# All modulation dot products moved beside tokens and filter spectra, and each slot of the joined stage reordered: evictions and weights first, norm steps behind

## The chip, the cores and the metric

One core of a Trainium2 chip. The metric is the time of one launch in device microseconds (us), median of several executions. The kernel is one program of ten stages with a barrier of all engines between two stages; instructions of one engine run in the order written, and semaphores order the engines against each other.

## What is computed

Two transformer-like blocks on 1024 tokens of width 1024, in float32: a first block (16 meta tokens, a sparse attention, a gated recurrence, an output product, a layer norm), then a block with latent attention over the tokens and 256 context rows, then one with long convolutions whose filters are made on the fly and transformed to spectra. What matters here:

```
a  = silu(gate_proj(h)) * features            # per unit "G"
x  = layer_norm(alpha*h + a @ w_out)          # units "OUT", chain norm1
shift, scale, gate = silu(c) @ ada_w[i] + ada_b[i]     # i = 0, 1: 48 columns of 128
a2 = rmsnorm(x)*g*(1+scale) + shift           # chain norm2, needs the modulation
ac = the same for the context rows with silu(c_ctx)    # i = 0 only
cq, ckv, k_rope, gate = split(a2 @ mla_w_in)  # then rmsnorm of cq and ckv, q, k, v
spec = rfft(filters * decay)                  # independent of everything above
```

The modulation is 48 dot products per partition: `ada_w[:, m, :]` is a 128 x 1024 tile (512 KB), and tile m against the condition row gives column m of `K.ada`. The first 16 columns are needed for the context rows too, which makes 64 products.

## The kernel before

**Stage one, `stage_spectra_tokens` (line 449).** TensorE multiplies the tokens with two small weights, tile by tile (9 tiles, `token_products`, lines 711 and 713), then makes the filters (`hidden_out`, line 736) and transforms them (line 766). The loop over `it` from 0 to 3 takes one order and one half of the channels; `it` is order-major (`o, h = it // 2, it % 2`). VectorE multiplies the filters with `decay` out of PSUM (line 632), forms radix sums (`radix`, lines 422 to 433), and takes the latents of each token tile (`take_latent`, 577 to 580, then `norm_latents`, 584 to 592). ScalarE makes `decay`, 8 tiles of 128 x 1024 (line 665), empties the value banks (672) and the spectrum banks (688) into a ring of four tiles `kst`. The sync queue (SP) stores values (537), spectra (550), and in `it == 3` reloads the block's input, one of 8 pieces beside each of the first 8 spectrum stores (555). TensorE runs three steps ahead of the emptied banks; the transposes of the latents (723) wait for `normed`.

**The joined stage, `stage_gates_to_keys` (line 1727).** 141 units in one list `UNITS`, each one PSUM bank of products: units 0 to 7 `G` (gates of half 0), 8 to 15 `OUT`, 16 to 23 and 24 to 31 the same for half 1, 32 to 34 the context rows, 35 to 49 and 50 to 64 the input projections of both halves, from 65 (`QN`) on queries, keys and values. A unit of 8 k-tiles is 24 matmuls, three per k-tile (`split_product`, lines 313 to 315: float32 as two parts). Four banks turn over. Each unit has a weight tile of its own (`WeightStream`, line 1565): SP loads 512 KB into one of two raw slots, ScalarE rounds it (1592) once the unit two back is done, GpSimd subtracts to get the rest (1598), and TensorE waits for that. So per unit there is a fixed chain: products of unit u, then rounding and rest of tile u+2, and that has until the end of unit u+1.

The order of each engine's work is written out by hand: for every unit u ScalarE does first the norm steps listed for u, then empties unit u's bank, then rounds tile u+2; VectorE does the modulation work and norm steps of u, then its part of unit u; GpSimd does its adds for u, then the rest of tile u+2. Norm steps stand in `CHAIN` (norm1 and norm2 for each half, `HalfNorm`, line 1609: ScalarE squares, GpSimd adds, TensorE sums over partitions in `total`, line 1647, VectorE and ScalarE make the root): `center` 18 and 34, `sums1` 20 and 36, `sums2` 25 and 40, `apply` 27 to 31 and 41 to 45. TensorE comes to `total` right behind unit `sums1` or `sums2` and waits there for all seven adds.

The modulation (`AdaSums`, line 1676) stands in this stage: `A1` takes columns 0 to 15, in pairs (1 MB loads), with both conditions (lines 1717 and 1720) beside units 0 to 11, `A2` columns 16 to 47 beside units 49 to 64. SP's loads of the pairs stand between its loads of the weight tiles, and each waits for the pair two back.

Of the kernel before, what the change touches and what calls it, by code (L numbers as in the profile page):

```python
# [18 lines left out]
F32 = mybir.dt.float32  # L19
# [6 lines left out]
P = 128  # L26
# [421 lines left out]

def stage_spectra_tokens(K):

    nc, dram = K.nc, K.dram
    decay = K.view(1024, 8192).rearrange("p (t c) -> p t c", t=8)
# [5 lines left out]
    delta = K.view(23744, 1024)  # L458
# [25 lines left out]
    latents_out = K.sem("latents_stored")  # L484

# [25 lines left out]
    with nc.Block() as block:  # L511

        @block.sync
        def _(sp):
# [11 lines left out]
            for dst, src in [(w_fb[0:64, :, :, :], dram["filt_w_out"]),  # L526
                             (delta, bass.AP(dram["delta"].tensor, 0, [[0, P], [1, D]])), (K.ident, dram["ident"]),
                             (K.kvg_row, bass.AP(dram["kv_g_row"].tensor, 0, [[0, P], [1, P]]))]:
                sp.dma_start(dst, src).then_inc(loads, 16)
            sp.dma_start(mats[:, 0:NSPEC0 * P], dram["dft_spec"][:, 0:NSPEC0 * P]).then_inc(mats_loaded, 16)  # L530
# [16 lines left out]
            for n, (it, s, p, row, _) in enumerate(spec_order):  # L547

                sp.wait_ge(sp_ev, n + 1)
                sp.dma_start(dram["spec"][it, row, :, :], kst[:, n % 4, :]).then_inc(stored[n % 4], 16)  # L550
                if it == 3 and s == 0 and n % 17 < 8:

                    sp.wait_ge(hd_ev, 64)
                    k = n % 17
                    sp.dma_start(K.view(1024, 8 * E).rearrange("p (k n) -> p k n", k=8)[:, k, :],
                                 dram["hT"][:, k, :]).then_inc(h_loaded, 16)
# [5 lines left out]
        def _(dve):  # L562
# [5 lines left out]
            def make_weights():  # L568
                dve.wait_ge(loads, 16 * 4)
# [45 lines left out]
            for it in range(4):  # L615
                o, h = it // 2, it % 2
                for s in range(2):
                    if it == 0 and s == 1:

                        radix(K, dve, link, lambda t2: ed[:, 0, 2 * t2:2 * t2 + 2, :], Y[0], tmp, y_ready[0])  # L620
                        for t in range(1, 9):
                            take_latent(t)
                        norm_latents()
# [4 lines left out]
                    for t in range(TT):  # L628
                        dve.wait_ge(hd_mm, n + 1)
                        if n == 0:  # L630
                            dve.wait_ge(decay_ready, 1)
                        ins = v.tensor_tensor(ed[:, s, t, :], K.bank(n % 4),
                                              decay[:, t, h * HALF:(h + 1) * HALF], ALU.mult)
# [9 lines left out]
                for s in range(2):  # L643
# [5 lines left out]
                    radix(K, dve, link, lambda t2: ed[:, s, 2 * t2:2 * t2 + 2, :], Y[s], tmp, y_ready[s])  # L649

        @block.scalar
        def _(act):
# [9 lines left out]
            act.wait_ge(loads, 16 * 4)  # L662
# [3 lines left out]
            ins.then_inc(decay_ready, 1)  # L666
            for t in range(9):
# [9 lines left out]
            for n in range(len(spec_order)):  # L677
                if n == 3:
# [4 lines left out]
                    nc.scalar.activation(cT[:, L:E], K.bank(2, META), ACT.Copy).then_inc(t_ev, 1)  # L683
                act.wait_ge(sp_mm, n + 1)
# [6 lines left out]
        def _(pe):  # L691
# [34 lines left out]
            def hidden_out(it, parts=(0, 1)):  # L726
                o, h = it // 2, it % 2
# [881 lines left out]
class HalfNorm:  # L1609
# [3 lines left out]
    def __init__(self, K, tag, x, kt, dim, banks, sq, rstd, acc, widths=(HALF, HALF)):  # L1613
# [3 lines left out]
        self.sums = [K.bank(b, n) for b, n in zip(banks, widths)]  # L1617
# [27 lines left out]
    def total(self, pe, j):  # L1645
        pe.wait_ge(self.added, (self.kt - 1) * (j + 1))
        self.K.nc.tensor.matmul(self.sums[j], self.K.ones, self.acc[:, 0:self.widths[j]], start=True, stop=True)\  # L1647
# [26 lines left out]


class AdaSums:


    def __init__(self, K, tag, first, pairs, with_ctx, w_at, cond_at, sums_at, spare=None):
        self.spare = spare  # L1680
        self.K, self.first, self.pairs, self.with_ctx = K, first, pairs, with_ctx
        self.w = [K.view(w_at + 2048 * s, 2048).rearrange("p (t k) -> p t k", t=2) for s in range(2)]
        self.cond = [K.view(cond_at + D * n, D) for n in range(2)]
        self.both = K.view(cond_at, 2 * D)
        self.sums = [K.view(sums_at + 4 * s, 4).rearrange("p (t v) -> p t v", v=2) for s in range(2)]
        self.rows_in, self.rows_ready = K.sem(f"{tag}_conditions_loaded"), K.sem(f"{tag}_conditions_ready")
        self.loaded = [K.sem(f"{tag}_ada_loaded{s}") for s in range(2)]
        self.used, self.ctx_used, self.copied = (K.sem(f"{tag}_ada_{n}") for n in ("used", "ctx_used", "copied"))

    def load_rows(self, sp):  # L1690
        sp.dma_start(self.both, bass.AP(self.K.dram["cond"].tensor, 0, [[0, P], [1, 2 * D]])).then_inc(self.rows_in, 16)

    def silu(self, act):
        act.wait_ge(self.rows_in, 16)
        self.K.nc.scalar.activation(self.both, self.both, ACT.Silu).then_inc(self.rows_ready, 1)

    def load(self, sp, g):
        if g < self.pairs:
            if g >= 2:
                sp.wait_ge(self.used, 2 * (g - 1))  # L1700
            at = self.first + 2 * g
            sp.dma_start(self.w[g % 2], self.K.dram["ada_w"][:, at:at + 2, :]).then_inc(self.loaded[g % 2], 16)

    def work(self, dve, g):
        v = self.K.nc.vector
        at, sums = self.first + 2 * g, self.sums[g % 2]
# [1608 lines left out]
```

## Time and profile before

| | us |
|---|---|
| median of 3 runs | 3032.46 (3028.85 to 3034.70) |
| profiled execution, its time | 3030.52 |
| its span, first to last instruction | 3028.7 |
| PE busy in it | 2740.2 (90%) |
| DVE busy in it | 1878.6 (62%) |
| mean granted TensorE clock | 0.953 |

Times below count from the start of the span. Stage one runs from 0 to 376, the joined stage from 1081. In the views PE is TensorE, DVE VectorE, ACT ScalarE, POOL GpSimd, SP the sync queue. A row of the order of time has the start, the duration, engine, line, operation, names, and in brackets how long the engine was idle before it and what ended that. The profile names PEclk the granted clock, in shares of 2.4 GHz.

### The profile page before, as it was taken

What the parts mean: (1) busy time and instruction counts of PE and PEld (TensorE: products, weight loads), DVE (VectorE), ACT (ScalarE), POOL (GpSimd) and SP (SyncE); (2) the same over time, 40 slices, a digit from 0 to 9 for tenths busy, and PEclk for the clock granted to TensorE, in tenths of its full rate; (3) what the DMA queues carried; (4) which work ended last, traced back from release to release, by engine and by line L of the source; (5) the groups of instructions that cost most, each with busy time, mean ns of one, the idle gap of its engine ahead of it and who ended that gap; (6) DMA issues with size and microseconds to landing.
All of it is one profiled execution on the core that took longest, in us unless ns stands there. A gap on an engine that the chain in (4) does not pass through costs nothing. (4 is left out here: it accounts for less than half of the span.)

```text
span 3028.7 us, 30579 instructions
## 1 busy us (share of the span) xinstructions
PE 2740.2 (90%) x11377; PEld 1868.9 (62%) x11377; DVE 1878.6 (62%) x2979; ACT 894.8 (30%) x1519; POOL 810.6 (27%) x486
## 2 busy tenths in 40 slices
PE   7999989978689978788999999996999998999967
PEld 3544434547456556566778899995778885444456
DVE  6256239999576668755851555554785533888564
ACT  2111121100344332435434565552332211111122
POOL 0000000004021135565432233324542220343234
PEclk9999999989889989899999999997999999999979
DMA  4211411110100034143856323214421123111043
GB/s 151 81 70 63 142 62 42 35 43 1 56 1 1 1 146 160 63 142 127 280 188 206 93 57 91 68 38 134 144 84 49 42 70 149 59 59 59 28 167 111
DMA packets 109560, 269.78 MB, mean 89 GB/s; under 512 B 18464, under 2 KB 34664, under 8 KB 105001
## 3 DMA queue, kind: packets, MB, share of 16 engines
q1 hardware_dynamic: 109418, 267.90, 26.5%
q8 instruction: 88, 1.44, 0.2%
q14 instruction: 54, 0.44, 0.0%
HBM read 206.87 MB, written 60.99 MB: 88 GB/s over the span
## 5 line engine op out<-in xcount | busy, mean ns | idle before, releaser
L313 PE MATMUL psum<-part,part 128*128 128x512 f32 (+1 forms) x1984 | 766.9, 387 | 94.4 <-POOL part L1598 49.2
L314 PE MATMUL psum<-part,part 128*128 128x512 f32 (+1 forms) x1984 | 744.4, 375 | 0.0
L315 PE MATMUL psum<-part,part 128*128 128x512 f32 (+1 forms) x1984 | 742.9, 374 | 0.0
L1598 POOL TENSOR_TENSOR part<-arena,part 128x1024 fp32r<-128x1024 f32 (+1 forms) x149 | 370.8, 2489 | 712.3 <-ACT part L1592 712.3
L313 PEld LDWEIGHTS psum<-part,part 128*128 128x128 f32 x1984 | 379.8, 191 | 183.4 <-POOL part L1598 95.5
L314 PEld LDWEIGHTS psum<-part,part 128*128 128x128 f32 x1984 | 380.4, 192 | 71.3 <-issue 3.2
L315 PEld LDWEIGHTS psum<-part,part 128*128 128x128 f32 x1984 | 379.2, 191 | 71.6
L221 PE MATMUL psum<-arena 128*128 128x512 f32 (+1 forms) x672 | 232.4, 505 | 17.3 <-DMA arena<-in_w_f 10.0
L1592 ACT ACTIVATE part<-arena 128x1024 fp32r<-128x1024 f32 (+1 forms) x149 | 155.4, 1043 | 262.9 <-PE psum L315 183.0
L1135 POOL TENSOR_TENSOR arena<-arena 128x256 f32<-128x256 f32 x56 | 38.2, 682 | 705.2 <-PE psum L1148 705.2
L2413 DVE TENSOR_REDUCE arena<-psum 128x1 f32<-128x1280 f32 x64 | 95.5, 1492 | 175.9 <-PE psum L2365 175.9
L766 PE MATMUL psum<-arena 128*128 128x512 f32 x464 | 200.6, 593 | 0.7 <-issue 0.7
L221 PEld LDWEIGHTS psum<-arena 128*128 128x128 f32 x672 | 114.3, 193 | 136.0 <-issue 127.9
L2887 PE MATMUL psum<-arena 128*128 128x512 f32 x448 | 192.9, 592 | 0.0
L920 DVE TENSOR_SCALAR_CACHE_REDUCE arena<-arena 128x384 bf16<-128x384 f32 (+2 forms) x198 | 173.9, 940 | 1.9 <-PEq L100 0.8
L766 PEld LDWEIGHTS psum<-arena 128*128 128x128 f32 x464 | 87.7, 190 | 112.7 <-issue 112.7
L2887 PEld LDWEIGHTS psum<-arena 128*128 128x128 f32 x448 | 85.1, 190 | 107.1 <-issue 107.1
L2873 PE MATMUL psum<-arena 128*128 128x512 f32 x256 | 118.5, 623 | 27.4 <-DVE arena L2974 14.2
L2454 ACT ACTIVATE part<-psum 128x512 fp32r<-128x512 f32 (+1 forms) x192 | 93.6, 522 | 134.5 <-PE psum L2374 134.4
L2426 DVE TENSOR_TENSOR part<-psum,part 128x512 fp32r<-128x512 f32 (+1 forms) x192 | 109.1, 595 | 37.3 <-ACT part L2454 37.3
L2902 ACT ACTIVATE arena<-psum 128x512 f32<-128x512 f32 x64 | 36.1, 599 | 301.7 <-POOL arena L2996 174.0
L2873 PEld LDWEIGHTS psum<-arena 128*128 128x128 f32 x256 | 50.7, 200 | 94.4 <-issue 80.8
(311 smaller groups left out, 4074.4 us busy)
## 6 DMA issues: line engine op xcount, KB each, us to landing
arena<-in_ada_w SPq DMA_DIRECT2D x24, 1024.0 KB, 5.3
arena<-in_w_hy SPq DMA_DIRECT2D x40, 512.0 KB, 3.2
scratch_spec<-arena SPq DMA_DIRECT2D x68, 256.0 KB, 2.0
arena<-scratch_spec SPq DMA_DIRECT2D x12, 1024.0 KB, 5.3
arena<-in_w_gate SPq DMA_DIRECT2D x16, 512.0 KB, 4.1
arena<-in_w_out SPq DMA_DIRECT2D x16, 512.0 KB, 4.0
arena<-in_w_mgate SPq DMA_DIRECT2D x16, 512.0 KB, 4.1
arena<-in_w_mout SPq DMA_DIRECT2D x16, 512.0 KB, 3.5
```

Source lines behind the costliest of these rows:

```text
L221: last = nc.tensor.matmul(acc, slot_w[s][:, c], rhs(k, n0, n), start=(k == 0), stop=(k == kt - 1))
L313: nc.tensor.matmul(acc, a_hi, b_hi, start=start, stop=False)
L314: nc.tensor.matmul(acc, a_hi, b_lo, start=False, stop=False)
L315: return nc.tensor.matmul(acc, a_lo, b_hi, start=False, stop=stop)
L766: last = nc.tensor.matmul(K.bank(4 + n % 4), mats[:, m * P:(m + 1) * P], Y[s][:, y, :], start=(q == 0), stop=(q == len(blocks) - 1))
L920: last = v.tensor_scalar(junk[:, (block_at(n + 2) - block_at(2)):(block_at(n + 3) - block_at(2))], s, against if isinstance(against, float ...
L1592: self.K.nc.scalar.activation(self.hi[i % 2][:, 0:n], self.raw[i % 2][:, 0:n], ACT.Copy)\
L1598: self.K.nc.gpsimd.tensor_tensor(self.lo[s][:, 0:n], self.raw[s][:, 0:n], self.hi[s][:, 0:n].bitcast(F32), ALU.subtract).then_inc(self.spl ...
L2413: v.reduce_max(top[:, i % 2:i % 2 + 1], K.psum[:, at:at + LC], AX_X).then_inc(topped, 1)
L2426: v.tensor_tensor(pT_lo[g % 2][:, k0:k0 + cnt, cols], chunk_bank(n, cnt).rearrange("p (k n) -> p k n", n=P), pT_hi[g % 2][:, k0:k0 + cnt, ...
L2873: last = nc.tensor.matmul(K.bank(4 * (g % 2) + b), fwd[:, m * P:(m + 1) * P], tile(it, PAIRS[n], part), start=(part == 0), stop=(part == 1))
L2887: last = nc.tensor.matmul(K.bank(n), inv[:, m * P:(m + 1) * P], tile(it, r, part), start=(q == 0), stop=(q == len(blocks) - 1))
```

## The change

Three parts.

**Modulation into stage one.** `AdaSums` is rewritten: one class, single columns (512 KB loads, two slots at 7168 and 8192), sums written straight into `K.ada`. Columns 0 to 23 (0 to 15 with both conditions) are worked on VectorE beside token tiles 1 to 8, three per tile behind that tile's `take_latent`: five products of 128 x 1024. `norm_latents` stays behind them. Columns 24 to 47 are worked behind the radix sums of `it` = 1, 2 and 3 (7, 7 and 10 of them). SP issues each load behind a value store or a spectrum store, and waits first for the column two back. The condition rows (1 MB) and two columns are loaded before the first DFT matrices. The bias and the three `modA` vectors are made at the end of the stage. To make room, `decay` is 8 tiles of 128 x 512 and made twice: for channels of half 0 at the start, for half 1 at spectrum n = 18 (16 activations of 256 columns), and the loop over `it` is half-major. In `it == 3` input pieces 0 to 2 are loaded beside the first three stores, pieces 3 to 7 beside the last five (n % 17 from 12 on), behind the last column.

**Modulation out of the joined stage.** A1, A2, their loads, the condition rows and `modulated` go. `NC` (the context norm) is scaled at units 12 and 13 and rounded at 29 and 30 instead of 13 and 16.

**The slots of the joined stage.** For every u each engine now empties unit u (or does its part of it) and rounds or subtracts tile u+2 first, and does the norm steps of u behind that. The numbers in `CHAIN` go down: by one for `center`, `stats1`, `scale`, and the centring is split over two units; by two for `sums2` of half 0, `stats2` and `apply` of half 0. `total` of norm1 comes behind unit 19 and 35 instead of 20 and 36, of norm2 behind 23 and 39 instead of 25 and 40.

```
 def stage_spectra_tokens(K):
-    decay = K.view(1024, 8192).rearrange("p (t c) -> p t c", t=8)
+    decay = K.view(1024, 4096).rearrange("p (t c) -> p t c", t=8)
+    A = AdaSums(K, [m for t in range(8) for m in (2 * t, 2 * t + 1, 16 + t)] + list(range(24, 48)), 16, (7168, 8192),
+                5120, K.view(45568, D))
+    ADA_LATE = {1: range(24, 31), 2: range(31, 38), 3: range(38, 48)}
...                                   # SP
+            A.load_rows(sp)
+            A.load(sp, 0)
+            A.load(sp, 1)
             sp.dma_start(mats[:, 0:NSPEC0 * P], dram["dft_spec"][:, 0:NSPEC0 * P]).then_inc(mats_loaded, 16)
...
                 sp.dma_start(dram["vN"][0:n, t, :], vN_slot[t % 3][0:n, :]).then_inc(v_out[t % 3], 16)
+                if t:
+                    for i in range(3 * t - 3, 3 * t):
+                        A.load(sp, i + 2)
...
+                late = ADA_LATE.get(it, [])
+                if 2 <= n % 17 < 2 + len(late):
+                    A.load(sp, late[n % 17 - 2] + 2)
+                if it == 3:
+                    ks = [n % 17] if n % 17 < 3 else [n % 17 - 9] if 12 <= n % 17 < 17 else []
+                    for k in ks:
+                        sp.wait_ge(hd_ev, 64)
+                        if k >= 3:
+                            sp.wait_ge(A.used, 48)
...                                   # VectorE
                         for t in range(1, 9):
                             take_latent(t)
+                            for i in range(3 * t - 3, 3 * t):
+                                A.work(dve, i)
                         norm_latents()
...
                     radix(K, dve, link, lambda t2: ed[:, s, 2 * t2:2 * t2 + 2, :], Y[s], tmp, y_ready[s])
+                for i in ADA_LATE.get(it, []):
+                    A.work(dve, i)
 def stage_gates_to_keys(K):
-    CHAIN = {0: dict(center=18, sums1=20, stats1=21, scale={21: [0, 1], 22: [2, 3, 4], 23: [5, 6, 7]}, sums2=25, stats2=26,
-                     apply={27: [0], 28: [1, 2], 29: [3, 4], 30: [5, 6], 31: [7]},
-                     add1={18: [1, 2, 3], 19: [4, 5, 6, 7]}, add2={22: [1], 23: [2, 3, 4], 24: [5, 6, 7]}),
+    CHAIN = {0: dict(mean=17, center={17: [0, 1, 2, 3], 18: [4, 5, 6, 7]}, sums1=19, stats1=20,
+                     scale={20: [0, 1], 21: [2, 3, 4], 22: [5, 6, 7]}, sums2=23, stats2=24,
+                     apply={24: [0], 25: [1, 2], 26: [3, 4], 27: [5, 6], 28: [7]},
+                     add1={17: [1, 2, 3], 18: [4, 5, 6, 7]}, add2={20: [1], 21: [2, 3, 4], 22: [5, 6, 7]}),
...
```

## Rows read from the trace of the kernel before

**Rows 1.** Busy time of each engine in three stretches of the joined stage.

```profile
core 0: us, PE busy (x) PEld busy (x) DVE busy (x) ACT busy (x) POOL busy (x), PEclk, DMA share, GB/s
1090.00:1218.00 128.00, 110.42 (x434) 86.66 (x435) 116.69 (x143) 42.90 (x63) 67.33 (x32) 0.91 0.45 163
1218.00:1328.70 110.70, 89.67 (x343) 69.20 (x342) 80.72 (x65) 44.52 (x58) 63.25 (x33) 0.89 0.26 81
...
1391.00:1545.00 154.00, 144.32 (x589) 112.30 (x589) 129.41 (x126) 69.93 (x91) 70.49 (x31) 0.97 0.67 230
```

**Rows 2.** Waits of PE, joined stage: us in total, times, longest.

```profile
PE psum L313 <- POOL part L1598: 45.3, 20, 6.1
PE psum L313 <- DVE part L2109: 11.7, 2, 9.6
```

**Rows 3.** PE in order of time: two rows of steady work, 42 matmuls apart.

```profile
1107.44 0.40 PE L313 MATMUL psum<-part,part 128*128 128x512 f32 x1
...
1117.20 0.39 PE L313 MATMUL psum<-part,part 128*128 128x512 f32 x1
```

**Rows 4.** PE in order of time: units 14, 20, 23 and 36 start after a wait.

```profile
1193.60 0.79 PE L313 MATMUL psum<-part,part 128*128 128x512 f32 x1 [5.75 <-POOL part L1598]
...
1236.28 0.80 PE L313 MATMUL psum<-part,part 128*128 128x512 f32 x1 [6.09 <-POOL part L1598]
...
1262.48 0.79 PE L313 MATMUL psum<-part,part 128*128 128x512 f32 x1 [5.98 <-POOL part L1598]
...
1353.19 0.79 PE L313 MATMUL psum<-part,part 128*128 128x512 f32 x1 [5.66 <-POOL part L1598]
```

**Rows 5.** Dot products, and rests of weights: duration min/median/max in ns.

```profile
L1720 DVE CUSTOM_DVE_ANT_0 arena<-arena x48: 1212/1226/3469, 1103.3 to 1548.5; 128x1024 f32<-128x1024 f32 x48
...
L1598 POOL TENSOR_TENSOR part<-arena,part x149: 1851/2409/3385, 1086.9 to 3000.9; 128x1024 fp32r<-128x1024 f32 x141, 128x768 fp32r<-128x768 f32 x8
```

**Rows 6.** In order of time, half 0's norm1: unit 17 emptied, squares, adds, sum.

```profile
1218.26 0.60 ACT L2072 ACTIVATE arena<-psum 128x512 f32<-128x512 f32 x1 [3.95 <-PE psum L315]
...
1224.23 2.44 ACT L1627 ACTIVATE arena<-arena 128x512 f32<-128x512 f32 x4 [4.42 <-DVE arena L2153]
...
1236.19 6.55 POOL L1643 TENSOR_TENSOR arena<-arena 128x512 f32<-128x512 f32 x4
...
1243.24 1.02 PE L1647 MATMUL psum<-arena 128*128 128x512 f32 x2
```

**Rows 7.** Stage one in order of time, decay to the first transforms; then `it` = 2.

```profile
34.33 8.42 ACT L665 ACTIVATE arena<-arena 128x1024 f32<-128x1024 f32 x8
...
42.88 3.08 DVE L632 TENSOR_TENSOR arena<-psum,arena 128x512 f32<-128x512 f32 x5 [5.54 <-ACT arena L665]
...
62.41 1.22 DVE L433 SCALAR_TENSOR_TENSOR arena<-arena 128x1024 f32<-128x1024 f32 x1
...
121.14 0.16 DVE L577 TENSOR_SCALAR arena<-psum 128x4 f32<-128x4 f32 x1 [7.97 <-PE psum L711]
...
124.43 2.44 DVE L592 SCALAR_TENSOR_TENSOR arena<-arena 16x128 f32<-16x128 f32 x9
...
222.06 0.69 DVE L632 TENSOR_TENSOR arena<-psum,arena 128x512 f32<-128x512 f32 x1 [14.64 <-PE psum L736]
...
49.92 0.81 PE L711 MATMUL psum<-arena 128*128 128x132 f32 x2
...
122.62 5.39 PE L766 MATMUL psum<-arena 128*128 128x512 f32 x12 [0.73 <-issue]
...
129.03 7.03 PE L766 MATMUL psum<-arena 128*128 128x512 f32 x16
```

**Rows 8.** Loads of stage one: count, KB each, median us from issue to landing.

```profile
arena<-in_hT SPq DMA_DIRECT2D x15, 520.0 KB, 4.0
...
arena<-in_w_idx SPq DMA_DIRECT2D x2, 512.0 KB, 3.4
```

**Rows 9.** The end of stage one: SP's last spectrum stores, PE's next product.

```profile
363.18 10.62 SPq L550 DMA_DIRECT2D scratch_spec<-arena  x4
...
380.13 4.63 PE L221 MATMUL psum<-arena 128*128 128x512 f32 x5 [7.31 <-DMA arena<-in_w_idx]
```

More of the change, by code:

```diff
@@ L446, in chain, with __init__, load_rows, silu @@
     return link
+class AdaSums:
+    def __init__(self, K, order, with_ctx, w_at, cond_at, spare):
+        self.K, self.order, self.with_ctx, self.spare = K, order, with_ctx, spare
+        self.w = [K.view(at, D) for at in w_at]
+        self.cond = [K.view(cond_at + D * n, D) for n in range(2)]
+        self.both = K.view(cond_at, 2 * D)
+        self.rows_in, self.rows_ready = K.sem("ada_conditions_loaded"), K.sem("ada_conditions_ready")
+        self.loaded = [K.sem(f"ada_loaded{s}") for s in range(2)]
+        self.used, self.ctx_used = K.sem("ada_used"), K.sem("ada_ctx_used")
+    def load_rows(self, sp):
+        sp.dma_start(self.both, bass.AP(self.K.dram["cond"].tensor, 0, [[0, P], [1, 2 * D]])).then_inc(self.rows_in, 16)
+    def silu(self, act):
+        act.wait_ge(self.rows_in, 16)
+        self.K.nc.scalar.activation(self.both, self.both, ACT.Silu).then_inc(self.rows_ready, 1)
+    def load(self, sp, i):
+        if i < len(self.order):
+            if i >= 2:
+                sp.wait_ge(self.used, i - 1)
+            sp.dma_start(self.w[i % 2], self.K.dram["ada_w"][:, self.order[i], :]).then_inc(self.loaded[i % 2], 16)
+    def work(self, dve, i):
+        product = self.K.nc.vector.tensor_tensor_reduce
+        m, w = self.order[i], self.w[i % 2]
+        if i == 0:
+            dve.wait_ge(self.rows_ready, 1)
+        dve.wait_ge(self.loaded[i % 2], 16 * (i // 2 + 1))
+        if m < self.with_ctx:
+            n = sum(t < self.with_ctx for t in self.order[:i])
+            if n:
+                dve.wait_ge(self.ctx_used, n)
+            product(self.spare, w, self.cond[1], 1.0, 0.0, ALU.mult, ALU.add, self.K.ada[:, m, 1:2])\
+                .then_inc(self.ctx_used, 1)
+            dve.wait_ge(self.ctx_used, n + 1)
+        product(w, w, self.cond[0], 1.0, 0.0, ALU.mult, ALU.add, self.K.ada[:, m, 0:1]).then_inc(self.used, 1)
 def stage_spectra_tokens(K):
     nc, dram = K.nc, K.dram
-    decay = K.view(1024, 8192).rearrange("p (t c) -> p t c", t=8)
+    decay = K.view(1024, 4096).rearrange("p (t c) -> p t c", t=8)
     ed = K.view(9216, 8192).rearrange("p (s t c) -> p s t c", s=2, t=8)
@@ L683, in _ @@
                     nc.scalar.activation(cT[:, L:E], K.bank(2, META), ACT.Copy).then_inc(t_ev, 1)
+                if n == 18:
+                    act.wait_ge(hd_ev, 32)
+                    for t in range(TT):
+                        for q in range(2):
+                            ins = nc.scalar.activation(decay[:, t, 256 * q:256 * q + 256], delta_late[q], ACT.Exp,
+                                                       scale=K.col("neg_t", t))
+                    ins.then_inc(decay_ready, 1)
                 act.wait_ge(sp_mm, n + 1)
@@ L1616, in __init__ @@
         self.acc = K.view(acc, max(widths))
-        self.sums = [K.bank(b, n) for b, n in zip(banks, widths)]
+        self.banks, self.sums = banks, [K.bank(b, n) for b, n in zip(banks, widths)]
         self.rstd = [K.view(at, n) for at, n in zip(rstd, widths)]
@@ L1673, in __getitem__ @@
         return self.tiles[k][:, columns]
[L1676 to L1706, printed above, removed]
-        if g == 0:
-            dve.wait_ge(self.rows_ready, 1)
-        dve.wait_ge(self.loaded[g % 2], 16 * (g // 2 + 1))
-        if g >= 2:
-            dve.wait_ge(self.copied, g - 1)
-        for t in range(2):
-            w = self.w[g % 2][:, t, :]
-            if self.with_ctx:
-                if 2 * g + t:
-                    dve.wait_ge(self.ctx_used, 2 * g + t)
-                v.tensor_tensor_reduce(self.spare(g), w, self.cond[1], 1.0, 0.0, ALU.mult, ALU.add,
-                                       sums[:, t, 1:2]).then_inc(self.ctx_used, 1)
-                dve.wait_ge(self.ctx_used, 2 * g + t + 1)
-            v.tensor_tensor_reduce(w, w, self.cond[0], 1.0, 0.0, ALU.mult, ALU.add, sums[:, t, 0:1])\
-                .then_inc(self.used, 1)
-        dve.wait_ge(self.used, 2 * g + 2)
-        n = 2 if self.with_ctx else 1
-        v.tensor_copy(self.K.ada[:, at:at + 2, 0:n], sums[:, :, 0:n]).then_inc(self.copied, 1)
```

298 lines of the change are left out of this document (133 added, 165 removed).

## The prediction, made before the changed kernel ran

> **What bounds the kernel now.** I read first the busy time by stretches, and there the joined stage alone, since every edit but those in stage one lies in it. TensorE does a third of its work of the stage while units 0 to 17 run, and over 128.0 us it is busy 110.4; over units 18 to 31 it is busy 89.7 of 110.7, and from unit 41 to the queries 144.3 of 154.0, with granted clocks of 0.91, 0.89 and 0.97 [rows 1]. The steady pitch of a matmul is (1117.20 - 1107.44) / 42 = 0.2324 us [rows 3], so a unit of 24 is 5.58, units 0 to 17 are 100.4 and cost 128.0. The stage is bound by TensorE where it runs, but 27.6 us are lost in that stretch: 17.6 idle, 10.0 at the low clock. The waits say on whom: 45.3 us in 20 waits on GpSimd's rest of a weight tile [rows 2]. The order of time shows the second half of the price: behind a wait of 5 to 6 us the first matmul lasts 0.79 instead of 0.40 [rows 3, 4], the 1.2 GHz level. With some four such starts in 0 to 17 (start of the stage included) 10.0 us are 2.5 each.
>
> Why is the rest late? Not GpSimd: it is busy 67 of 128 us, VectorE 117 of 128 [rows 1]. A dot product takes 1.23 us, and 3.4 when it meets a rest of weights; a rest 2.4, up to 3.4 [rows 5]. SP waits for the dot products (two pairs back) before it issues the next weight load, so a late VectorE makes late weights.
>
> **Removing A1.** Nothing but gates and products is left beside units 0 to 15. A rest of tile u+2 ends about 0.6 + 1.0 + 2.4 = 4.0 us behind unit u by its chain, and TensorE wants it at 5.58: 1.6 to spare, 0.6 with a slow rest. I take all waits away but the first (weights and h must land). The wait of 11.7 - 9.6 = 2.1 at the second matmul group [rows 2] goes too: that weight tile stood behind 1 MB of condition rows. One cold start of 2.5 stays. Units 0 to 17 and two small sums: 100.4 + 2.5 + 1.0 = 103.9 against 128.0 + 0.7 for the sum that now comes one unit earlier: **-25**.
>
> **The slots.** I wrote both orders out as one list per engine. Before: norm steps of u, empty u, round u+2. After: empty u, round u+2, norm steps of u, and the numbers one lower. The lists come out the same. What really moves is what went down by more than one, or stayed behind: the centring is in two parts, so unit 18 is emptied between them, the context rounding leaves unit 16, `apply` comes sooner, and above all TensorE's `total` stands one unit sooner (norm1) or two and one (norm2). TensorE waits there for seven GpSimd adds.
>
> Half 0, norm1, from the end of unit 17 (unit 17 is emptied at 1218.3): squares begin 6 us later; the last four adds took 6.55 and ended at 1242.7, 24.5 later; the sum ran at 1243.24, right behind unit 20 [rows 6], so before it cost no wait. After: four squares are done at +8.7, unit 18 is emptied and tile 20 rounded at once, so GpSimd has no hole before rest 20; VectorE's second four centrings come behind unit 18's three operations, and the adds end between +20 (adds at 1.3, about half of a rest's 2.4 for half its columns [rows 5]) and +23 (at 1.64 as in the row). Unit 19 ends at +11.2. TensorE waits 9 to 12 us, starts cold, and ends unit 20 at 0.7 + 5.6 + 2.5 behind the sum, +29 to +32, where before unit 20 and its sum ended at +26 (1244.3). Tile 23 comes 19 us behind the end of unit 20 in both lists (1262.48 less 1243.2 [rows 4, 6]); `total` of norm2 waits some 9 us more at unit 23, and unit 24's start and wait of before go in exchange. From unit 20 on I make this even. Part: +3 to +6, I take **+4.5**, by the contended adds, which are those in the rows.
>
> Half 1, norm1: before, tile 36 was rounded behind all eight squares and unit 36 began at 1353.19 after 5.66 [rows 4]. After, it is rounded between them, but the sum stands ahead of unit 36 and its adds end about as late: +0.5. Norm2: `total` ahead of unit 40 waits about 5 us and leaves the clock low, where before one wait of 3 stood behind it: +4. Together +1.5 to +5.5, I take **+4.5**.
>
> From unit 41 on 9.7 us are idle and 3% of the clock is gone [rows 1]. The A2 products keep VectorE at 129 of 154 us and put 16 MB on the queue; without them I leave 4 us of waits for norm sums of three squares through two buffers: **-7.5**. Joined stage: -25 + 4.5 + 4.5 - 7.5 = -23.5.
>
> **Stage one.** The decay of one half takes half of 8.42 [rows 7], so VectorE's first multiply, which waited 5.54 for it, starts at 38.7 instead of 42.88. Then TensorE's eight filter products run on at full clock and end at 44.3, and the token tiles begin there instead of 49.92; with 2.4 us of low clock that go as well, tiles are 8.0 earlier. That is the gain, and the dot products take it back. VectorE's radix sums end at 63.6 - 5.7 = 57.9. Per tile there are five products, 2 x 2.48 + 1.15 = 6.1 us (five times the 1.226 of [rows 5]), under a tile of about 8.7 (7.97 idle + 0.7 [rows 7]). But two slots mean that a column is loaded only when the one two back is used. With a load of L the cycle of a tile is 4.96 + L. Rows bound L: 3.4 us for 512 KB, 4.0 for 520 KB beside stores [rows 8]; I take 3.5, since only one value store per tile is beside: 8.5, just under 8.7. So tile 8's latent is taken at 116.9 and column 23 ends at 125.4, where `norm_latents` began at 121.9. The last latent is normed at 130.4 instead of 124.43 + 2.44 = 126.9 [rows 7]. TensorE has three spectra in between (5.2 us), idles 3 and 5 us, and after the transposes starts cold; the products that began at 129.03 begin at 130.5 and cost 2.5 more: **+4** (L = 3.4: +3; L = 4.0: +7.8).
>
> In `it` = 1 and 2 seven columns need three loads in a row, some 3 x L + 4 = 15.7 us with L = 3.9 beside stores, in a hole of 14.64 [rows 7] where 1.6 more are covered by TensorE's four banks: 0 to 1 each, **+1**. SP holds a spectrum store back by up to 7 us there; the ring of four covers 10 (four outputs of 3.45 less the store). Spectrum work of 10 columns in `it` = 3 ends near 357, ahead of the input pieces at 360. The 16 small decay activations and three more table loads stand where ScalarE has over 2 us free per output.
>
> The end: the last store is issued at 373.8 [rows 9] and lands in 2.0. Now a 520 KB piece is issued behind it and lands in 4.0 [rows 8]; the barrier and the next stage's weights come 0.4 + 2.0 later: **+2.5**. Stage one: +7.5.
>
> **Sum.** -23.5 + 7.5 = -16 against the execution of 3030.5 (span 3028.7 and 1.8 around it), 3014.5; the median of the runs lies 2 above that execution, so 3016.5. I say 3016.
>
> **Two rules weighed.** Rows 4 show the low clock behind waits of 5.7 us and more. The Trainium skill (TensorE: Matmul & The Clock Gate, "HAM oscillation") says that an engine which waits between bursts starts each burst at the throttled clock; by that rule fewer but longer waits at the sums are worse than the short ones they replace. The trace agrees, and the 2.5 per sum is counted. Rows 5 show a product of 3.4 us beside a rest. The skill (SBUF — State Buffer, "Who interferes with whom") says that a VectorE operation with two SBUF inputs and a GpSimd one that reads SBUF exclude each other; by that rule the adds end at +23, without it at +20 and the sum would be 3013.
>
> **Rivals.**
> A, a smaller gain: sums wait for everything. Each term at its bad end: -25 + 6 + 5.5 - 4 and stage one 3.8 + 7.5, which is -6: 3026. For it: VectorE and GpSimd block each other in every row of norm1. Against: five ends at once. 14%.
> B, a larger gain: adds at 1.3 and L = 3.4: -25 + 2.5 + 1.5 - 9 + 6 = -24; 3008; where unit 24's wait is saved whole as well, 3002. 14%.
> C, slower: the two slots in stage one. If a load beside the stores lands at L, eight tiles, two times three loads and the end cost 7.5 + 8 (L - 3.5) + 6 (L - 3.9). It decides at L = 5.2, where +29 is more than the joined stage gives and leaves +6; at 5.6 it is +11, 3044. For it: SP issues loads only in turn behind stores. Against: medians of 3.4 and 4.0 [rows 8]. 10%.
> D, nothing: the joined stage's idle time was hidden work of norms, not of dot products; -25 falls to -10, 3031. Against: beside units 0 to 16 only the small context squares are norm work on ScalarE, and the 3.4 us products and SP's order meet every weight tile there [rows 5]. 6%.
>
> **How the numbers follow.** The forecast (3008 to 3024) has 56%. The range 2999 to 3032 takes in A, B and D and leaves C and far ends out. A measurement of this kernel can tell 0.2%, 6 us, from no change: faster 0.79 (forecast, B, most of A), same 0.11 (rest of A, D), slower 0.10 (C).
>
> **What the profile of after would show.** Right: units 0 to 17 in about 104 us with one wait; TensorE's longest waits of the stage, 9 to 12 us, at line of `total` on GpSimd's adds, each with a start at the low clock; no wait on GpSimd's rests beside units 0 to 16. In stage one TensorE idles about 8 us ahead of the transposes, and column products start on "DMA in_ada_w". Wrong: rests still late in units 0 to 17 (D), waits of TensorE on `hidden_out` of several us (C), sums that do not wait (B).

## The result, and the profile after

The changed kernel takes 3052.41 us in the median (3051.63 to 3052.62, four runs), beside 3031.12 for the kernel before (3028.85 to 3034.70): ratio 1.0071, 95% interval 1.0059 to 1.0083. It is 21 us slower; the prediction said 16 us faster. The profiled execution has a span of 3050.8 against 3028.7, which is 22.1 more.

I place the difference by landmarks of TensorE that both traces have. The first product behind stage one starts at 380.13 [rows 9] and now at 416.99: **+36.9**. The first product of the joined stage comes at 1089.98 and now at 1124.35, so the stages between have given 2.5 of that back, in code that is the same. This length is 709.9 us before, 707.4 after, and between 705.5 and 710.7 in the executions of the experiments below, so no effect of the change is shown in it. The joined stage, taken from there to the second weight tile of the first values (unit 121 of 141), went from 551.96 to 540.70 us: **-11.3**. Behind it 1.0 more goes.

The joined stage first: busy time by stretches, which end ahead of unit 18, of unit 35, of unit 41 and at the first values. The kernel before, in the boundaries that answer to these (its first stretch is as good as that of [rows 1]):

```profile
1218.20:1341.70 123.50, 99.24 (x417) 77.94 (x416) 87.84 (x70) 49.09 (x64) 74.92 (x38) 0.90 0.30 93
1341.70:1391.00 49.30, 39.10 (x149) 29.76 (x149) 17.38 (x19) 25.05 (x36) 34.25 (x21) 0.91 0.36 119
1391.00:1641.94 250.94, 240.18 (x1031) 191.55 (x1030) 152.76 (x163) 102.73 (x145) 93.51 (x42) 0.98 0.61 208
```

The same stretches of the changed kernel, with units 0 to 17 in the first line:

```profile
1124.35:1229.80 105.45, 104.38 (x437) 83.67 (x438) 63.25 (x60) 35.25 (x50) 59.81 (x32) 0.97 0.40 129
1229.80:1361.60 131.80, 98.78 (x415) 77.43 (x414) 90.47 (x81) 53.04 (x75) 73.69 (x39) 0.87 0.29 94
1361.60:1417.40 55.80, 41.00 (x149) 30.66 (x150) 15.64 (x14) 21.73 (x32) 33.97 (x20) 0.85 0.25 83
1417.40:1665.05 247.65, 238.30 (x1031) 191.26 (x1029) 85.80 (x82) 102.87 (x145) 89.72 (x42) 0.99 0.41 138
```

Units 0 to 17 fell from 128.2 to 105.45 us, by 22.8, with TensorE busy in all but 1.1 of it. Then two stretches grew, by 8.3 and 6.5, and the last lost 3.3. The waits of TensorE in the joined stage of the changed kernel (us in total, times, longest), where [rows 2] had 45.3 us on GpSimd's rests:

```profile
PE psum L1730 <- POOL arena L1724: 36.5, 6, 11.7
PE psum L313 <- POOL part L1679: 15.0, 8, 7.1
PE psum L313 <- DVE part L2120: 10.6, 2, 9.6
PE psum L1730 <- POOL arena L1721: 3.5, 2, 3.1
```

L1730 is `total`, L1724 the adds. Three of the four sums stand in order of time like this, behind units 19, 23 and 35:

```profile
1252.60 2.08 PE L1730 MATMUL psum<-arena 128*128 128x512 f32 x2 [11.67 <-POOL arena L1724]
1296.45 2.08 PE L1730 MATMUL psum<-arena 128*128 128x512 f32 x2 [8.99 <-POOL arena L1724]
1374.89 2.07 PE L1730 MATMUL psum<-arena 128*128 128x512 f32 x2 [7.47 <-POOL arena L1724]
```

Each lasts 2.08 instead of 1.02 [rows 6]: the 1.2 GHz level. Now stage one. TensorE in order of time, the changed kernel (L847 are the spectra, L804 the transposes, L817 the filter products of `hidden_out`):

```profile
120.82 6.80 PE L847 MATMUL psum<-arena 128*128 128x512 f32 x12 [6.55 <-DVE arena L638]
130.98 2.48 PE L804 MATMUL psum<-arena 16*128 16x16 f32 x9 [3.36 <-DVE arena L652]
133.26 9.05 PE L847 MATMUL psum<-arena 128*128 128x512 f32 x16
...
227.13 3.70 PE L817 MATMUL psum<-arena 64*128 64x512 f32 x8
232.85 20.85 PE L817 MATMUL psum<-arena 64*128 64x512 f32 x24 [2.02 <-DVE arena L694]
253.63 2.93 PE L847 MATMUL psum<-arena 128*128 128x512 f32 x3
...
305.15 3.70 PE L817 MATMUL psum<-arena 64*128 64x512 f32 x8
311.22 20.73 PE L817 MATMUL psum<-arena 64*128 64x512 f32 x24 [2.37 <-DVE arena L694]
...
416.99 8.49 PE L221 MATMUL psum<-arena 128*128 128x512 f32 x15 [9.36 <-DMA arena<-in_w_idx]
```

The filter products of `it` = 2 and 3 are what to look at. In the kernel before the same 32 matmuls are one row:

```profile
220.90 14.00 PE L736 MATMUL psum<-arena 64*128 64x512 f32 x32
```

After, eight run, TensorE waits 2.02 us for VectorE's multiply, and the 24 behind take 20.85 us, 0.87 each instead of 0.43. The busy time over them says the engine does not idle (20.60 of 20.60) and that the granted clock is 0.50, half of 2.4 GHz, all the way:

```profile
233.00:253.60 20.60, 20.60 (x24) 7.70 (x24) 9.87 (x15) 0.00 (x0) 0.00 (x0) 0.50 0.11 35
```

So a wait of 2 us costs 26.5 - 13.9 = 12.6. With the second (305.15 to 331.88, 26.7) these are 25 of the 36.9 us. The spectra behind each start at half clock too and take 51.59 and 75.75 us where the kernel before has 50.05 and 74.08, so the two waits cost 28.6 in all. And what made VectorE late, its last dot products of `it` = 1 in order of time:

```profile
213.84 1.23 DVE L488 CUSTOM_DVE_ANT_0 arena<-arena 128x1024 f32<-128x1024 f32 x1 [0.19 <-DVE arena L433]
...
224.41 1.23 DVE L488 CUSTOM_DVE_ANT_0 arena<-arena 128x1024 f32<-128x1024 f32 x1 [2.33 <-DMA arena<-in_ada_w]
...
230.96 1.23 DVE L488 CUSTOM_DVE_ANT_0 arena<-arena 128x1024 f32<-128x1024 f32 x1 [2.08 <-DMA arena<-in_ada_w]
...
232.11 2.48 DVE L694 TENSOR_TENSOR arena<-psum,arena 128x512 f32<-128x512 f32 x4
```

Seven products are 8.1 us of work, but from 213.84 to 232.11 they take 18.3, because each load waits for the slot two back. Issue to landing of the loads there (the window 210 to 240; then beside the token tiles, 85 to 130; last column the median in us):

```profile
arena<-in_ada_w SPq DMA_DIRECT2D x7, 512.0 KB, 4.8
...
arena<-in_ada_w SPq DMA_DIRECT2D x15, 512.0 KB, 3.6
```

### The profile page after: what moved, and what is told of

It reads as the page before. It is cut to its first block and busy times, and to the rows that moved or that the text cites. A ratio compares the mean times of both kernels' runs of the same rounds, so it can differ in the third digit from the quotient of the medians.

```text
span 3050.8 us, 30582 instructions
## 1 busy us (share of the span) xinstructions
PE 2754.4 (90%) x11377; PEld 1872.0 (61%) x11377; DVE 1836.9 (60%) x2954; ACT 897.4 (29%) x1536; POOL 799.4 (26%) x486
## 5 line engine op out<-in xcount | busy, mean ns | idle before, releaser
L847 PE MATMUL psum<-arena 128*128 128x512 f32 x464 | 207.2, 609 | 6.5 <-DVE arena L638 6.5
L2876 PE MATMUL psum<-arena 128*128 128x512 f32 x448 | 192.9, 592 | 0.0
L847 PEld LDWEIGHTS psum<-arena 128*128 128x128 f32 x464 | 90.4, 196 | 124.0 <-issue 116.7
L2862 PE MATMUL psum<-arena 128*128 128x512 f32 x256 | 119.7, 628 | 27.9 <-DVE arena L2963 14.5
```

Source lines behind the costliest of these rows:

```text
L847: last = nc.tensor.matmul(K.bank(4 + n % 4), mats[:, m * P:(m + 1) * P], Y[s][:, y, :], start=(q == 0), stop=(q == len(blocks) - 1))
L2862: last = nc.tensor.matmul(K.bank(4 * (g % 2) + b), fwd[:, m * P:(m + 1) * P], tile(it, PAIRS[n], part), start=(part == 0), stop=(part == 1))
L2876: last = nc.tensor.matmul(K.bank(n), inv[:, m * P:(m + 1) * P], tile(it, r, part), start=(q == 0), stop=(q == len(blocks) - 1))
```

## The experiments

Each kernel was timed beside the kernel before on the same chip; ratios are to that. Times of the kernel before differ between chips by up to 3 us in the median, so a ratio is safer than a difference of times.

### The sums one unit later

```
-    CHAIN = {0: dict(... sums1=19, stats1=20, ... sums2=23, stats2=24,
+    CHAIN = {0: dict(... sums1=20, stats1=20, ... sums2=24, stats2=24,
-             1: dict(... sums1=35, stats1=36, ... sums2=39, stats2=40,
+             1: dict(... sums1=36, stats1=36, ... sums2=40, stats2=40,
```

> Changed kernel with only the four places of `total` one unit later (behind units 20, 24, 36, 40; the norm steps stay in their slots). Theory 'early totals': TensorE stands at `total` for adds that end at a fixed time, so each wait shrinks by one unit of 5.6 us: 11.7 to 6, 9.0 to 3.4, 7.5 to 2, 4.7 to 0; the joined stage becomes 8 to 16 us shorter than the 540.7 us of the changed kernel. Rival 'the chain of the norm is what is late': what a sum no longer waits, the next rest or the next sum waits; the stage stays within 3 us.

Measured: ratio 1.0018 (1.0008 to 1.0028), so 16 us of the 21 are back. The joined stage is 521.6 us, 19.1 below the changed kernel:

```profile
1128.46:1356.90 228.44, 203.68 (x851) 161.32 (x851) 156.94 (x141) 88.52 (x125) 133.86 (x71) 0.94 0.34 111
1356.90:1403.20 46.30, 40.20 (x149) 31.11 (x150) 15.24 (x15) 22.68 (x33) 34.01 (x20) 0.89 0.31 103
1403.20:1650.08 246.88, 237.98 (x1032) 190.43 (x1030) 85.40 (x81) 102.20 (x145) 89.44 (x42) 0.99 0.42 141
```

Against 237.25, 55.8 and 247.65 these are 8.8, 9.5 and 0.8 less. The sum behind unit 20 in order of time, with what stands on both sides of it:

```profile
1250.02 0.79 PE L313 MATMUL psum<-part,part 128*128 128x512 f32 x1 [3.85 <-POOL part L1679]
1257.91 1.12 PE L1730 MATMUL psum<-arena 128*128 128x512 f32 x2 [0.61 <-POOL arena L1724]
1260.66 0.50 PE L313 MATMUL psum<-part,part 128*128 128x512 f32 x1 [1.62 <-POOL part L1679]
```

The wait of 11.67 is now 0.61, more than the unit moved: 3.85 stands ahead of unit 20 instead, on its weights' rest. GpSimd's last four adds ended 1252.5 - 1124.35 = 128.2 us into the stage in the changed kernel, and 1257.86 - 1128.46 = 129.4 here: the adds have their own time, and a unit put ahead of the sum fills the wait. The early-totals theory holds; it gave a little more than its range. The rival is right in part: 3.85 us are now waited for on the rest.

The same for the two norm1 sums alone (`sums1=20` and `36`, the others as changed):

> Changed kernel with only the two `total` of norm1 one unit later (behind units 20 and 36); those of norm2 stay behind 23 and 39. All four together gave 19.1 us in the joined stage, 8.8 of it by the start of unit 35 and 10.2 from there to the start of unit 41. If each sum is worth the same, this kernel has about half: joined stage 531 us, against 540.7 and 521.6. If norm1 alone sets it (the norm2 sum waits for a chain that starts at the norm1 sum), all of it: 523. If norm2 alone: 539.

Measured: ratio 1.0036 (1.0024 to 1.0049), joined stage 1650.83 - 1125.05 = 525.8 us. That is 14.9 of the 19.1: the norm1 sums carry most of it, between the first and the second case of what was expected. The norm2 sums still wait 9.17 and 4.67 us, and moving them too brings 4 more.

### Fewer columns ahead of the filter products

```
-    ADA_LATE = {1: range(24, 31), 2: range(31, 38), 3: range(38, 48)}
+    ADA_LATE = {1: range(24, 29), 2: range(29, 34), 3: range(34, 44)}
...
+            link(v.memset(K.ada[:, 44:48, :], 0.0))
```

> Changed kernel with five instead of seven columns behind the radix sums of it = 1 and of it = 2; four of the 48 columns (44 to 47) are left out and set to zero, so this part of the modulation is missing. Theory 'a short wait costs the clock': the fifth product ends at 225.7, ahead of TensorE's filter products at 227.1, so no wait of 2.0 and 2.4 us and no low clock there: the 32 matmuls take 13.9 instead of 26.5 us each time, the next stage begins 24 to 27 us sooner, time 3026 to 3029. Rival 'the wait is worth its length': 4 to 5 us sooner, 3048. Rival 'loads beside the filter products lower the clock': the matmuls stay at 1.2 GHz.

Measured: ratio 0.9992 (0.9982 to 1.0001), 24 us below the changed kernel's 1.0071. The filter products of `it` = 2 and 3, and the next stage's first product:

```profile
225.48 14.00 PE L818 MATMUL psum<-arena 64*128 64x512 f32 x32
...
289.38 14.00 PE L818 MATMUL psum<-arena 64*128 64x512 f32 x32
...
387.34 33.09 PE L221 MATMUL psum<-arena 128*128 128x512 f32 x73 [9.95 <-DMA arena<-in_w_idx]
```

No wait and no low clock, and 387.34 is 29.7 ahead of 416.99: the 28.6 of the two waits, and a token phase that was 1.7 quicker in this execution, less 0.6 of a longer last wait. The rival that took the wait at its length asked for 4 to 5. The rival of the loads falls too: five of seven loads still stand there, and the clock is full.

### One wait, put into the kernel before

```
                        if n == 0:
                            dve.wait_ge(decay_ready, 1)
+                       if n == 16:
+                           for _ in range(4):
+                               link(v.tensor_tensor(tmp[0], tmp[0], tmp[1], ALU.mult))
```

> Kernel before, with four additional VectorE operations of 128x1024 (4.6 us) ahead of the first multiply of it = 1 and nothing else. TensorE's four banks cover 3.5 us, so it should wait 2 to 3 us once. Theory 'the clock falls at the wait and stays low as long as products with 64 rows of weights follow': 24 to 28 matmuls at 0.87 instead of 0.43 us each, the stretch costs 12 to 14 us, time 3043 to 3045. Rival 'a cold start as everywhere else in this kernel': wait plus 2.5, time 3036. Rival 'the wait is absorbed later': no change.

Measured: 3044.74 beside 3027.89, ratio 1.0054 (1.0035 to 1.0073), which is 16 us.

```profile
156.87 3.70 PE L739 MATMUL psum<-arena 64*128 64x512 f32 x8
163.81 20.78 PE L739 MATMUL psum<-arena 64*128 64x512 f32 x24 [3.25 <-DVE arena L635]
184.52 11.76 PE L769 MATMUL psum<-arena 128*128 128x512 f32 x23
```

From 156.87 to 184.52 are 27.65 us against 13.9: one wait of 3.25 costs 13.7. No dot product and no column load exists here, so neither is needed for it. The row behind has 23 matmuls of 128 rows in 11.76 us, 1.8 more than their full pace of 0.434 each: the clock comes back within that row, as it had not in the 20.78 us ahead of it.

The kernel before has such a wait of its own, at `it` = 0, where VectorE waits for `decay`. Two rows of its order of time, which overlap by a matmul:

```profile
43.63 2.09 PE L736 MATMUL psum<-arena 64*128 64x512 f32 x3 [2.52 <-DVE arena L632]
44.66 5.32 PE L736 MATMUL psum<-arena 64*128 64x512 f32 x6
```

Behind a wait of 2.52 the products of 64 rows run at 0.88 us each (granted clock 0.50 from 45 to 50), and the first token products behind them at half pace until 54.4. The eight lose 2.8 us and the tokens 2.4, so this low clock costs 5.2, twice the 2.5 of a start in the joined stage.

### 128 rows instead of 64

```
+            link(v.memset(w_ed[64:128, :, :, :], 0.0))
+            link(v.memset(hid[64:128, :], 0.0))
...
-                        nc.tensor.matmul(K.bank(n % 4), hid[0:64, t * P:(t + 1) * P],
-                                         w_ed[0:64, o, s, h * HALF:(h + 1) * HALF],
+                        nc.tensor.matmul(K.bank(n % 4), hid[:, t * P:(t + 1) * P],
+                                         w_ed[:, o, s, h * HALF:(h + 1) * HALF],
```

> Changed kernel with the filter products' contraction padded from 64 to 128 rows by zeros (zeros written to both operands in the first microseconds); everything else, with its waits of 2.0 and 2.4 us, stays. Theory 'rows of weights decide': behind the wait the matmuls start at 1.2 GHz and are back at 2.4 after some 5 us, so each stretch costs 2 + 2.5 instead of 12.6: 16 us less, 3036. Rival 'the form of the product (one start and stop per bank, VectorE's pace) or the DMA traffic decides': all 24 matmuls stay at 0.87 us, 3052. Rival 'zero rows don't count': the same as that.

Measured: ratio 1.0007 (0.9994 to 1.0021), 19 us below the changed kernel.

```profile
230.25 10.57 PE L819 MATMUL psum<-arena 128*128 128x512 f32 x24 [1.50 <-DVE arena L696]
...
297.04 12.26 PE L819 MATMUL psum<-arena 128*128 128x512 f32 x24 [3.01 <-DVE arena L696]
```

A wait of 1.5 leaves the clock where it is (10.57 is what 24 take at full clock), one of 3.0 costs 1.7 behind it. Form, banks, VectorE's pace and DMA traffic are those of the changed kernel; only rows of zeros came in. Waits differ from 2.02 and 2.37 by the luck of the loads, so I measured a row of waits in the kernel before, without loads, ahead of `it` = 1, 2 and 3:

```
+                       for _ in range({16: 2, 32: 3, 48: 5}.get(n, 0)):
+                           link(v.tensor_tensor(tmp[0], tmp[0], tmp[1], ALU.mult))
```

With 64 rows:

> Kernel before with VectorE held back ahead of the filter products of it = 1, 2, 3 by 2, 3 and 5 operations of 1.25 us. Four gave a wait of 3.25, so these should give waits of 0.75, 2.0 and 4.5 us. Theory 'any wait of two us and more drops the clock for the rest of the 64-row products': the 24 matmuls behind the wait take 10.4 us at the first, 20.8 at the second and third; 5.5 + 12.4 and 4.5 + 10.4 us longer in stage one, 28 us in all. Rival 'the drop has to do with something else of it = 1': other values.

```profile
161.27 18.34 PE L738 MATMUL psum<-arena 64*128 64x512 f32 x24 [0.73 <-DVE arena L634]
...
237.56 19.52 PE L738 MATMUL psum<-arena 64*128 64x512 f32 x24 [1.99 <-DVE arena L634]
...
316.37 20.84 PE L738 MATMUL psum<-arena 64*128 64x512 f32 x24 [4.50 <-DVE arena L634]
```

With 128 rows (the same edit and the padding above):

> The same three waits in the kernel before, with the filter products padded to 128 rows. Theory 'rows of weights decide how long the clock stays low': behind 0.75 us nothing, behind 2.0 and 4.5 us the 24 matmuls take 10.4 plus 0 to 2.5 us. Rival 'the changed kernel was a special case': 20.8 us behind 4.5.

```profile
158.54 10.57 PE L740 MATMUL psum<-arena 128*128 128x512 f32 x24 [0.73 <-DVE arena L636]
...
224.31 10.57 PE L740 MATMUL psum<-arena 128*128 128x512 f32 x24 [1.99 <-DVE arena L636]
...
292.60 13.61 PE L740 MATMUL psum<-arena 128*128 128x512 f32 x24 [4.50 <-DVE arena L636]
```

Three pairs, equal waits to the hundredth. Wait and low clock together cost, over the 10.6 us that a row of 24 lasts at full clock: 8.5, 10.9 and 14.8 us with 64 rows, 0.7, 2.0 and 7.5 with 128. The ratios are 1.0136 (1.0112 to 1.0160) and 1.0020 (1.0009 to 1.0030): 41 and 6 us by the medians' scale, where the rows above add up to 34 and 10. The traces have the difference. With 64 rows the spectra behind the three waits still start at half clock and take 52.41, 51.23 and 76.15 us for 50.05, 50.05 and 74.08: 5.6 more. With 128 rows the token products behind the wait at `it` = 0 have the full clock at once, and all that follows is 2.4 us ahead (133.62 against 136.00 for the second filter products). The next stage begins 40.8 and 7.5 us later than in the kernel before. Of the expectation one thing failed: 0.73 us was to cost nothing at 64 rows, and it cost almost as much as 2. There is no safe wait among those tried.

### No column at all

Loads and products of all 48 columns are taken out and the sums set to zero, which leaves the modulation out of the result; the halved decay, the half-major order and the places of the input pieces stay.

```
-    ADA_LATE = {1: range(24, 31), 2: range(31, 38), 3: range(38, 48)}
+    ADA_LATE = {}
...
-                            for i in range(3 * t - 3, 3 * t):
-                                A.work(dve, i)
```

> Changed kernel with no dot product at all: no column loads, no products, the 48 sums are set to zero (so the whole modulation is missing); halved decay, half-major order, input pieces and the joined stage stay as changed. Theory 'the columns cost all of it': without them the gain of the halved decay (7.7 us on the token tiles) is seen alone, and the next stage begins at 372 to 375 instead of 417.0 (before: 380.1), time 42 to 45 us below the changed kernel, ratio to before 0.993. Rival 'order and decay cost something themselves' (16 small activations, spectra stored in another order, input pieces late): the next stage begins behind 380, ratio 0.995 or more.

Measured: ratio 0.9946 (0.9930 to 0.9961), the next stage's first product at 373.53, between the two cases in the ratio but plainly the first by place. The filter products of `it` = 0's odd half start at 127.55, where the kernel before had 136.00 and the changed one 142.24: the halved decay gives 8.45, and the token tiles' columns take 14.7.

### The columns in six holes

In the kernel before VectorE idles in two places of a round: 14.6 us behind the odd radix sums, which the change filled with seven columns, and 11.3 behind the even ones, which it left empty.

```
+    ADA_HOLES = {(it, s): range(18 + 10 * (it - 1) + 5 * s, 23 + 10 * (it - 1) + 5 * s) for it in (1, 2, 3) for s in (0, 1)}
...
+        for where, i in zip((12, 12, 14, 14, 16) if s == 0 else (3, 3, 5, 5, 7), items):
+            ADA_LOADS.setdefault(17 * (it - 1 + s) + where, []).append(i + 2)
...
-                if t:
+                if 1 <= t <= 6:
...
-                    ks = [n % 17] if n % 17 < 3 else [n % 17 - 9] if 12 <= n % 17 < 17 else []
+                    ks = [n % 17] if n % 17 < 3 else [n % 17 - 6] if 9 <= n % 17 < 14 else []
...
-                            for i in range(3 * t - 3, 3 * t):
+                            for i in range(3 * t - 3, 3 * t if t <= 6 else 0):
...
                     radix(K, dve, link, lambda t2: ed[:, s, 2 * t2:2 * t2 + 2, :], Y[s], tmp, y_ready[s])
+                    for i in ADA_HOLES.get((it, s), []):
+                        A.work(dve, i)
```

> Changed kernel, all 48 columns, placed otherwise: 18 beside token tiles 1 to 6, none beside 7 and 8, so the latents are normed 9 us sooner; then five in each of six holes, behind the even and behind the odd radix sums of it = 1, 2, 3; SP loads two at a time; input pieces 3 to 7 from the tenth output of it = 3 on. Theory 'VectorE had the room, only the places were wrong': no TensorE wait at the filter products, one short one ahead of the transposes, next stage at 374 to 379 instead of 417, ratio to before 0.993 to 0.995. Rival 'the loads don't fit': the fifth column of the first hole is late, the odd radix sums begin late, TensorE waits there in each of three rounds and starts cold, next stage at 385 to 395.

Measured: ratio 0.9934 (0.9919 to 0.9949), 20 us faster than the kernel before with all the work done. TensorE's rows behind the tokens, and the next stage's first product:

```profile
114.30 5.39 PE L850 MATMUL psum<-arena 128*128 128x512 f32 x12 [0.73 <-issue]
119.62 1.25 PE L807 MATMUL psum<-arena 16*128 16x16 f32 x9
120.71 7.03 PE L850 MATMUL psum<-arena 128*128 128x512 f32 x16
...
371.81 42.91 PE L221 MATMUL psum<-arena 128*128 128x512 f32 x96 [7.32 <-DMA arena<-in_w_idx]
```

371.81 is even ahead of the kernel that computes no column (373.53), by the wait of 7.32 against 9.16: here the last input piece is not behind the last spectrum store. VectorE had the room.

### Together

The changed kernel with both small cures, the later sums and the padding:

> Changed kernel with both one-line cures: `total` one unit later in four places, and the filter products padded to 128 rows. If the two are independent, 16 and 20 us off the changed kernel: ratio to before 1.0071 - 0.0053 - 0.0064 = 0.995. Rival 'they share a limit': 0.999 or more.

Measured: 3012.77 beside 3030.07, ratio 0.9937 (0.9924 to 0.9951). They add up.

The columns in six holes, the later sums and the padding, all as above:

> Columns in two holes per round, sums one unit later, 128 rows. By the theory stage one ends as in the kernel with the two holes alone, since no filter product waits any more and the padding has nothing to cure; 16 us more come from the sums: ratio to before 0.988 to 0.990, 32 us below the kernel before. Rival 'padding costs something itself' (writing zeros, weights of 128 rows): 2 to 5 us less gain.

Measured: 2988.88 beside 3030.07, ratio **0.9862** (0.9847 to 0.9877), 41 us faster than before and 63 below the changed kernel. The gain is larger than both cases expected. The next stage begins at 370.19, so the padding costs nothing; the joined stage takes 1597.09 - 1078.11 = 519.0 us.

## Why the prediction was wrong

It asked for -16 and got +22 in the profiled execution: 38 us. By its own terms:

| term | predicted | measured |
|---|---|---|
| stage one, token phase | +4 | +6.2 |
| stage one, `it` = 1 and 2 | +1 | +26.9 |
| stage one, end | +2.5 | +3.7 |
| stages between | 0 | -2.5 |
| units 0 to 17 | -25 | -22.8 |
| half 0, sums | +4.5 | +8.3 |
| half 1, sums | +4.5 | +6.5 |
| from unit 41 on | -7.5 | -3.3 |
| behind the first values | 0 | -1.0 |

**The step that failed** is "in `it` = 1 and 2 seven columns need three loads in a row, some 3 x L + 4 = 15.7 us ... 0 to 1 each". Its first half was right in form: with the measured L of 4.8 the formula gives 18.4, and VectorE took 18.3. The hole and the banks cover 16.2, so the wait of 2.0 follows. What failed was the price of a wait, its own length. I had counted a low clock of 2.5 us behind each sum in the joined stage, but none here, and 2.5 would have been wrong as well: behind this wait it is 10.4, since every matmul up to the next product with 128 rows runs at 1.2 GHz. The 26.9 of the table are 12.6 and 12.8 for the two waits with their 24 products, and 1.5 in the spectra behind the first. The waits added to the kernel before (3.25 us costing 13.7) and the five-column kernel (24 us back) both show it. The trace of before had a row that could have warned: at `it` = 0 the filter products wait 2.52 and the low clock behind it costs 5.2 (shown above). The prediction used that stretch, where it books 2.4 us of low clock as part of the gain of the halved decay, but did not ask what such a wait would cost at `it` = 2 and 3, where 24 products of 64 rows stand behind it.

**Rival C** had the right place (two slots in stage one, a chance of 10%) and the wrong price: its formula with the measured 3.6 and 4.8 gives 7.5 + 0.8 + 5.4 = 13.7, and it should not have decided below L = 5.2. With the low clock in it, it decides at L = 4.1, where 3 x L + 4 passes 16.2.

**Token phase.** The gain was right (8.0 against 8.45). The cycle of a tile was 4.96 + L with 3.5, 8.5; it came out at 8.8 to 9.2, with L = 3.6 and 0.9 to 1.3 us of issue ahead of each tile's first product that I did not have. The forecast also let the products behind the transposes begin at 130.5, as soon as the last latent is normed, with no time for the transposes themselves (130.98 to 133.26 here). The last column ends at 129.66 instead of 125.4, and the last norm at 132.9 instead of 130.4. The two idle times of TensorE (3 and 5 forecast, 6.55 and 3.36 measured) and the cold start (9.05 for 16 matmuls, 7.03 before) are as described.

**End.** "Spectrum work of 10 columns in `it` = 3 ends near 357" is plainly wrong: the odd radix sums begin at 357.9, since they wait for TensorE, and the columns run from 370.2 to 399.2. It cost little, because the last piece stood behind the last store anyway; the wait for it is 2.05 us longer than before (9.36 against 7.31), and the other 1.7 of the 3.7 are the low clock behind the second wait.

**Units 0 to 17.** 105.45 for 103.9, no wait on a rest, D refuted. Two thirds of those 1.55 us are the second start: TensorE's wait there fell from 2.12 to 1.07, not to nothing, since what it waits for is VectorE's subtraction at L2120, not the queue alone. The prediction's opening remark that TensorE does a third of its work of the stage there is a misreading: it is 110.6 of 489.2 us of busy time up to the first values, less than a quarter. No term rests on it.

**Sums.** The row-by-row forecast held: adds end 22.7 us behind unit 17 (20 to 23 forecast), unit 20 ends at +31.5 (29 to 32), waits of 11.7, 9.0 and 4.7 for 9 to 12, 9, and 5 (the 7.5 behind unit 35 had no figure). The size was wrong where I called the rest even: from unit 20's end to unit 35 the changed kernel is 2.8 us slower, and half 0 costs 8.3 in place of 3 to 6. And I took as given that a sum one unit earlier has to wait; the experiment shows that each such unit was simply given away, 19 us in all. The order "total behind unit `sums1`" was in the diff, with the slot of `stats1` one later: nothing needed the sum that soon.

**From unit 41 on** I left 4 us of waits for norm sums, and 7.3 remain (2.25, 0.41, 1.47 and 3.13). The kernel before had 7.0 there too. Of its 9.7 us of idle time only 2.7 were waits on rests, and these fell to 1.0: the dot products there had been better hidden than I thought.

Of the rules weighed, the oscillation rule told the sign of the longer waits rightly. Its neighbour in the Trainium skill (TensorE: Matmul & The Clock Gate, "What's actually happening") says that being busy releases the throttle. The trace agrees for 128 rows (13.61 behind a wait of 4.5, so 3.0 us lost and then full clock) and does not for 64 rows: 20.8 us without a gap, all at 0.50.

## What to carry to other kernels

Ask of every stretch that TensorE runs without reserve which matmuls follow a possible wait: if their weights fill half of the rows, as here, price the wait at its length plus the whole of what follows at half clock, or pad them with zeros to 128 rows, which took no time here. Where one engine's work fills a hole of another, count the chain of its loads through its slots, not its busy time (8.1 us of products took 18.3), and look for other holes of the same round before filling one to the brim. Put a reduction that TensorE must do behind the unit that ends last before it is needed, not behind the one that its inputs are hoped to meet.

## What the runs showed of the hardware that I had not expected

- After a wait, 64-row float32 products of 512 columns keep TensorE at half clock while it is busy without a gap: 24 matmuls in 20.8 us at a granted clock of 0.50, in the changed kernel's two stretches and behind waits of 3.25 and 4.50 us; behind 1.99 and 0.73 they took 19.52 and 18.34. There the granted clock is still 1.00 for the first 2.4 us behind 0.73 and 0.98 for the first 1.4 behind 1.99, and then 0.50 while the engine is busy. Without a wait the same products hold the full clock for 14 us, at `it` = 1, 2 and 3 of the kernel before.
- With rows of zeros added to 128, waits of 0.73, 1.50 and 1.99 us left no trace (10.57), 2.48, 2.60 and 3.01 cost 1.6, 1.7 and 1.7 and 4.50 cost 3.0 beyond themselves. The added rows held only zeros. Why the rows matter no run here tells. Whether another number of rows between would do, and whether it is the rows of the weights or of the moving operand, wasn't tried: both were padded.
